# A Trainium2 layer kernel: its neighbourhood attention in units of one head and two query rows, on 64x64 and 64-column tiles of TensorE, with probabilities divided by GpSimd before they are transposed

## The reference

```python
def row_block(r):
    rs = r_start[r]          # clip(r - 4, 0, 32 - 8)
    ...
    s_loc = jnp.einsum('bjhd,bajchd->bhjac', q_r, k_r).astype(jnp.float32) * scale + bias.astype(jnp.float32)
    s_ctx = jnp.einsum('bjhd,blhd->bhjl', q_r, k_ctx).astype(jnp.float32) * scale
    s = jnp.concatenate([s_loc.reshape(b_, h_, GRID_W, n_loc), s_ctx], axis=-1)
    p = jax.nn.softmax(s, axis=-1).astype(v.dtype)
    p_loc = p[..., :n_loc].reshape(b_, h_, GRID_W, kr, WIN_C)
    return (jnp.einsum('bhjac,bajchd->bjhd', p_loc, v_r)
            + jnp.einsum('bhjl,blhd->bjhd', p[..., n_loc:], v_ctx))
```

## Time and profile before

| | before |
|---|---|
| median of 3 runs | 3817.42 us (3816.41 to 3820.98) |
| profiled execution, span from first to last instruction | 3823.5 us |
| profiled execution, own time beside the span | not given |
| TensorE busy in it | 3659.4 us, 96% |
| VectorE, ScalarE, GpSimd busy | 61%, 43%, 22% |

### The profile page before, as it was taken

How to read it: one execution, slowest core, us unless ns; L and a number is a source line. 1 busy time by engine, 2 the same in 40 slices (tenths; PEclk the granted TensorE clock), 3 DMA queues, 4 the chain that set the end, 5 groups by cost and what they waited for, 6 DMA issues and landing times. The chain is left out here.

```text
span 3823.5 us, 58042 instructions
## 1 busy us (share of the span) xinstructions
PE 3659.4 (96%) x19520; PEld 2936.9 (77%) x19520; DVE 2323.0 (61%) x3546; ACT 1645.7 (43%) x3006; POOL 856.0 (22%) x812
## 2 busy tenths in 40 slices
PE   8999999999997999989999999996799999999998
PEld 3444459986777999968888888785688888888887
DVE  4655632555656999953534353444767777677775
ACT  4333333334654666642424332322344445444452
POOL 3888500011106666610000000000000010000100
PEclk9999999999999999989999999997899999999999
DMA  7455455131115433344535352443477676766763
GB/s 283 155 144 142 119 182 130 57 86 45 26 46 183 125 118 122 96 160 125 177 105 170 99 172 73 152 154 130 145 214 226 214 220 206 214 224 215 219 209 92
DMA packets 258768, 570.97 MB, mean 149 GB/s; under 512 B 38971, under 2 KB 117339, under 8 KB 256347
## 3 DMA queue, kind: packets, MB, share of 16 engines
q1 hardware_dynamic: 225612, 451.18, 37.2%
q0 software_dynamic: 33040, 118.25, 10.4%
HBM read 458.27 MB, written 100.73 MB: 146 GB/s over the span
## 5 line engine op out<-in xcount | busy, mean ns | idle before, releaser
L3072 DVE TENSOR_TENSOR sb_we_low<-sb_we,sb_we_high 128x1024 fp32r<-128x1024 f32 x384 | 466.6, 1223 | 121.5 <-ACT sb_we_high L3023 121.5
L3023 ACT ACTIVATE sb_we_high<-sb_we 128x1024 fp32r<-128x1024 f32 x377 | 392.2, 1048 | 142.3 <-PE ey L2987 142.3
L2430 DVE TENSOR_TENSOR sb_wm_low<-sb_wm,sb_wm_high 128x1024 fp32r<-128x1024 f32 x127 | 155.4, 1224 | 393.6 <-ACT sb_wm_high L2340 393.6
L344 PE MATMUL p_ps<-sb_hT,sb_ring 128*128 128x512 f32 (+1 forms) x960 | 373.2, 549 | 0.0
L344 PEld LDWEIGHTS p_ps<-sb_hT,sb_ring 128*128 128x128 f32 x960 | 181.9, 190 | 186.2 <-issue 181.3
L2281 PE MATMUL pg<-sb_hb_high,sb_wm_high 128*128 128x512 f32 x768 | 303.3, 395 | 8.7 <-DVEq L2402 4.6
L2282 PE MATMUL pg<-sb_hb_low,sb_wm_high 128*128 128x512 f32 x768 | 300.4, 391 | 0.0
L2283 PE MATMUL pg<-sb_hb_high,sb_wm_low 128*128 128x512 f32 x768 | 300.1, 391 | 0.0
L2970 PE MATMUL eg<-sb_xe_parts,sb_we_high 128*128 128x512 f32 x1024 | 260.5, 396 | 1.6 <-DVE sb_xe_parts L3067 1.6
L2970 PE MATMUL eu<-sb_xe_parts,sb_we_high 128*128 128x512 f32 x1024 | 259.1, 395 | 0.0
L2932 POOL DMA_INDIRECT out<-sb_ybe,sb_ti x32 | 51.0, 1595 | 880.7 <-DVE sb_ybe L3107 822.7
(11 more groups left out here) (418 smaller groups left out, 8675.7 us busy)
## 6 DMA issues: line engine op xcount, KB each, us to landing
sb_we<-in_w_ex SPq DMA_DIRECT2D x384, 512.0 KB, 4.5
sb_wm<-in_w_gates SPq DMA_DIRECT2D x96, 512.0 KB, 3.6
sb_stage<-in_w_mod_row POOLq DMA_DIRECT2D x64, 256.0 KB, 3.6
sb_stage<-h_d SPq DMA_DIRECT2D x32, 512.0 KB, 4.3
sb_wm<-in_w_br SPq DMA_DIRECT2D x32, 512.0 KB
sb_ring<-in_w_ch POOLq DMA_DIRECT2D x19, 512.0 KB, 5.2
sb_gr<-gc_d SPq DMA_DIRECT2D x36, 256.0 KB, 3.8
sb_lk<-k_d SPq DMA_DIRECT2D x36, 256.0 KB, 4.0
```

Of the source, the lines that this page charges most:

```text
L344: last = nc.tensor.matmul(ps[:, b % BANKS, 0:wd], w[:, kind, k], hT[:, k, t0:t0 + wd], start=(k == 0), stop=(k == KD - 1))
L2430: v.tensor_tensor(wl[n], w[n], wh[n], ALU.subtract).then_inc(s.wl, 1)
L3023: nc.scalar.activation(wh[:, n % CUT], w[:, n % RAW], ACT.Copy).then_inc(s.wh, 1)
L3072: v.tensor_tensor(wl[:, n % CUT], w[:, n % RAW], wh[:, n % CUT], ALU.subtract).then_inc(s.wl, 1)
```

## The change

A unit becomes one head and two grid rows of queries (`j` = 0, 1); four units, the heads, make a pair of rows, and TensorE works on two of them, a pair `p` of heads, at a time. There are again 64 units, in 32 pairs, all unrolled. For each pair:

- `scores`: the queries go in as they are, as weights of 64 channels x 64 queries. A matmul for each head (`e`, partitions 64 e to 64 e + 63 of the input) and row (`j`, partitions 64 j to 64 j + 63 of the output), once for the local keys (512 columns, each row with its own window) and once for the context (256). GpSimd's doubled queries go.
- The scores are made negative (the query norm's factor and the bias table change sign), so that the maximum becomes a minimum. VectorE's `local` adds the bias and keeps the minimum in one instruction (in two halves where the two rows have different windows), `context` does the same for the context scores with a zero, straight from PSUM, and starts from the minimum of `local`. The exponential is taken in place with scale -1.
- GpSimd multiplies the 768 probabilities by the reciprocal of their sum (`sa.nm`), and TensorE's transposes wait for that.
- `turn`: four transposes for each unit into `turned`, then two each for the context of both units into `ctx_turned`. ScalarE copies the former (`copy_pt`), VectorE the latter for both units in one (`copy_ctx`).
- `values`: the values are the weights (128 keys x 64 channels) and the transposed probabilities of one row move (64 columns), so that the output comes out with its channels on partitions: 24 instructions a unit. The output's transposes, the scaling and the copies of quadrants go; ScalarE makes one copy a pair (`out`).
- There are four buffers for scores instead of two and two; the bias table holds each head for both rows (eight loads instead of four, four additions of the mask instead of two); a pair of grid rows is stored by two DMAs.
- `inner(0)` stands before the last pair's values.

The diff, cut to what is added; what it replaces stands in the functions above, and lines marked with a minus are kept where they are short:

```diff
@@ -671,11 +671,13 @@
...
+    UNITS = ROWS // 2 * H
+    PAIRS = UNITS // 2
...
+    BUF = 4
+    LK = KT - CT
@@ -685,53 +687,27 @@
...
+    def rows_of_unit(U):
+        i = U // 4
+        starts = [min(max(r - WR // 2, 0), ROWS - WR) for r in (2 * i, 2 * i + 1)]
+        return i, starts, [WR - 1 - (2 * i + j - starts[j]) for j in range(2)]
+    def edge(U):
+        _, _, shifts = rows_of_unit(U)
+        return shifts[0] != shifts[1]
+    def added(U):
+        return sum(2 if edge(x) else 1 for x in range(U))
...
+        area = sbuf(nc, c, "area", [P, 4976])
...
+        mx = sbuf(nc, c, "mx", [P, BUF, 4])
+        none = sbuf(nc, c, "none", [P, 1])
@@ -740,10 +716,11 @@
...
+        oc = sbuf(nc, c, "aoT", [P, 2, H, GRID])
...
+        sa = sems(nc, c, "at", "pad z zero rp sk bt0 sc lm cm ex rc nm tp tpc pt ptc o oe st0 st1")
@@ -772,10 +749,8 @@
...
+        sb = flat_ring[:, 0:BUF * KEYS].rearrange("p (u k) -> p u k", u=BUF)
+        bt = area[:, 1136:4976].rearrange("p (a r c) -> p a r c", a=H, c=GRID)
@@ -784,6 +759,7 @@
...
+        pt = FREE[:, 14336:14336 + 2 * KEYS].rearrange("p (u n c) -> p u n c", u=2, n=KT)
@@ -797,7 +773,8 @@
...
+        loc, cx, turned, po = bank[:, 0:2], bank[:, 2:4, 0:CTX], bank[:, 4:6], bank[:, 7, 0:2 * GRID].rearrange("p (u t) -> p u t", u=2)
+        ctx_turned = bank[:, 6].rearrange("p (u n c) -> p u n c", u=2, n=CT)
@@ -829,8 +806,8 @@
...
-                    half = h % 2
-                    sp.dma_start(bt[half * GRID:(half + 1) * GRID, h // 2], src).then_inc(sa.bt0, 16)
+                    for j in range(2):
+                        sp.dma_start(bt[j * GRID:(j + 1) * GRID, h], src).then_inc(sa.bt0, 16)
@@ -842,16 +819,16 @@
...
-                dst = g.oc_d.rearrange("(q p) (r t) -> p r q t", q=HP, t=GRID)
...
-                def store(i, odd):
-                    r = 2 * i + odd
-                    sp.wait_ge(sa.ote, 2 * (4 * i + 2 * odd + 2))
-                    sp.dma_start(dst[:, bass.ds(r, 1)].rearrange("p r q t -> p (r q) t"), oc[:, odd]).then_inc(s_st[odd], 16)
+                dst = g.oc_d.rearrange("(h c) (r t) -> c r h t", c=DH, t=GRID)
+                def store(i):
+                    sp.wait_ge(sa.oe, 2 * (i + 1))
+                    for j in range(2):
+                        sp.dma_start(dst[:, 2 * i + j], oc[j * DH:(j + 1) * DH, i % 2]).then_inc(s_st[i % 2], 16)
...
+                    store(n)
@@ -864,6 +841,7 @@
...
+                nc.gpsimd.memset(none[:], 0.0).then_inc(sa.zero, 1)
@@ -877,17 +855,10 @@
...
+                for U in range(UNITS):
+                    u = U % BUF
+                    pool.wait_ge(sa.rc, U + 1)
+                    nc.gpsimd.tensor_scalar(sb[:, u], sb[:, u], mx[:, u, 3:4], 1.0, ALU.mult, ALU.mult).then_inc(sa.nm, 1)
@@ -977,57 +948,59 @@
...
+                def scores(p):
+                    i, starts, _ = rows_of_unit(2 * p)
+                    hp = p % 2
+                    wait(pe, sa.lm, added(2 * p))
+                    for e in range(2):
+                        half = slice(e * DH, (e + 1) * DH)
+                        for j in range(2):
+                            at = CTX + starts[j] * GRID
+                            nc.tensor.matmul(loc[j * GRID:(j + 1) * GRID, e, 0:LOC], g.qn[half, hp, (2 * i + j) * GRID:(2 * i + j + 1) * GRID],
+                                             g.kn[half, hp, at:at + LOC], start=True, stop=True)
+                    if p == 0:
...
+                    wait(pe, sa.cm, 2 * p)
+                    for e in range(2):
+                        half = slice(e * DH, (e + 1) * DH)
+                        for j in range(2):
+                            nc.tensor.matmul(cx[j * GRID:(j + 1) * GRID, e], g.qn[half, hp, (2 * i + j) * GRID:(2 * i + j + 1) * GRID],
+                                             g.kn[half, hp, 0:CTX], start=True, stop=True).then_inc(sa.sc, 1)
+                def turn(p):
+                    for e in range(2):
+                        U = 2 * p + e
+                        pe.wait_ge(sa.nm, U + 1)
+                        for n in range(LK):
+                            last = nc.tensor.transpose(turned[:, e, n * P:(n + 1) * P], sb[:, U % BUF, n * P:(n + 1) * P], g.ident)
...
+                    for e in range(2):
+                        for n in range(CT):
+                            at = (LK + n) * P
+                            last = nc.tensor.transpose(ctx_turned[:, e, n], sb[:, (2 * p + e) % BUF, at:at + P], g.ident)
+                    last.then_inc(sa.tpc, 1)
+                def values(p):
+                    pe.wait_ge(sa.ptc, p + 1)
+                    wait(pe, sa.oe, p)
+                    for e in range(2):
+                        U = 2 * p + e
+                        _, starts, _ = rows_of_unit(U)
+                        cols = slice(U % 4 * DH, (U % 4 + 1) * DH)
+                        pe.wait_ge(sa.pt, U + 1)
+                        for n in range(KT):
+                            for j in range(2):
+                                rs = starts[j]
+                                if n >= LK:
+                                    v = vb[:, n - LK, cols]
+                                elif rs % 2:
+                                    v = v1[:, rs // 2 + n, cols]
+                                else:
+                                    v = vb[:, CT + rs // 2 + n, cols]
+                                last = nc.tensor.matmul(po[j * DH:(j + 1) * DH, e], v, pt[:, e, n, j * GRID:(j + 1) * GRID],
+                                                        start=(n == 0), stop=(n == KT - 1))
+                                if n == KT - 1 and e == 1:
+                                    last.then_inc(sa.o, 1)
@@ -1071,17 +1044,20 @@
...
+                scores(0)
+                scores(1)
...
+                for p in range(PAIRS):
+                    turn(p)
+                    if p + 2 < PAIRS:
+                        scores(p + 2)
+                    if p == PAIRS - 1:
+                        pe.wait_ge(sf.re, 16 * 2 * N2)
+                        pe.wait_ge(sa.cm, UNITS)
+                        inner(0)
+                    values(p)
@@ -1143,49 +1119,22 @@
...
+                def exps(U):
+                    act.wait_ge(sa.cm, U + 1)
+                    a(sb[:, U % BUF], sb[:, U % BUF], ACT.Exp, bias=mx[:, U % BUF, 1:2], scale=-1.0,
+                      accum_out=mx[:, U % BUF, 2:3]).then_inc(sa.ex, 1)
+                def copy_pt(U):
+                    act.wait_ge(sa.tp, U + 1)
+                    wait(act, sa.o, 2 * (U // 2))
+                    a(pt[:, U % 2, 0:LK], turned[:, U % 2].rearrange("p (n c) -> p n c", c=P), ACT.Copy).then_inc(sa.pt, 1)
+                def out(p):
+                    i, hp = p // 2, p % 2
+                    act.wait_ge(sa.o, 2 * (p + 1))
+                    if hp == 0:
+                        wait(act, s_st[i % 2], 32 * (i // 2))
+                    a(oc[:, i % 2, 2 * hp:2 * hp + 2], po, ACT.Copy).then_inc(sa.oe, 1)
@@ -1241,14 +1190,20 @@
...
+                for U in range(3):
+                    exps(U)
...
+                for p in range(PAIRS):
+                    copy_pt(2 * p)
+                    copy_pt(2 * p + 1)
+                    if p > 0:
+                        out(p - 1)
+                    for U in (2 * p + 3, 2 * p + 4):
+                        if U < UNITS:
+                            exps(U)
...
+                out(PAIRS - 1)
@@ -1323,7 +1278,7 @@
...
-                        v.tensor_scalar(nw[:, 0:1], nw[:, 0:1], DH ** -0.5, None, ALU.mult).then_inc(sm.rec, 1)
+                        v.tensor_scalar(nw[:, 0:1], nw[:, 0:1], -DH ** -0.5, None, ALU.mult).then_inc(sm.rec, 1)
@@ -1338,32 +1293,35 @@
...
+                def local(U):
+                    u = U % BUF
+                    _, _, shifts = rows_of_unit(U)
+                    dve.wait_ge(sa.sc, 4 * (U // 2 + 1))
+                    wait(dve, sa.tpc, (U - BUF) // 2 + 1)
+                    parts = [(0, P, shifts[0])] if not edge(U) else [(j * GRID, (j + 1) * GRID, shifts[j]) for j in range(2)]
+                    for lo, hi, dr in parts:
+                        v.tensor_tensor_reduce(sb[lo:hi, u, 0:LOC], loc[lo:hi, U % 2, 0:LOC], bt[lo:hi, U % 4, dr:dr + WR].rearrange("p r c -> p (r c)"),
+                                               1.0, 3e38, ALU.add, ALU.min, mx[lo:hi, u, 0:1]).then_inc(sa.lm, 1)
+                def context(U):
+                    u = U % BUF
+                    dve.wait_ge(sa.lm, added(U + 1))
+                    v.tensor_tensor_reduce(sb[:, u, LOC:KEYS], cx[:, U % 2], none[:].broadcast_to([P, CTX]),
+                                           1.0, mx[:, u, 0:1], ALU.add, ALU.min, mx[:, u, 1:2]).then_inc(sa.cm, 1)
+                def inverse_sum(U):
+                    u = U % BUF
...
                     v.reciprocal(mx[:, u, 3:4], mx[:, u, 2:3]).then_inc(sa.rc, 1)
...
+                def copy_ctx(p):
+                    dve.wait_ge(sa.tpc, p + 1)
```

(69 more changed lines are left out.)

146 lines of the change are left out of this document (1 added, 145 removed).

## The result

| | before | after |
|---|---|---|
| median, on the same chip, 4 runs each | 3818.62 us (3816.41 to 3820.98) | 3750.01 us (3745.48 to 3753.30) |
| profiled execution, own time | not given | 3748.97 us |
| its span | 3823.5 us | 3747.4 us |
| first matmul of the stage behind the attention | 1166.59 us | 1095.96 us |

The ratio is 0.9817, with a 95% interval of 0.9805 to 0.9829: 68.6 us, or 1.8%, **faster**. All of the gain is in the attention: the next stage's first matmul comes 70.6 us earlier. (The granted clock, averaged over the span, is 0.977 before and 0.976 after.)

The account below looks back on a forecast made before the run. It took TensorE to bound the kernel before and the ring to set the new pace: 32 x 8.26 = 264 against 243, 21 us more, plus 4 at the start, on 3817.4, gives 3842 us; range 3772 to 3885.

Parts of the forecast that it names:

- The ring: Waits through TensorE's transposes and scores, VectorE's logits and reciprocal, GpSimd's multiply: sets the pace, 2.90 + S + G = 8.26 us a pair.
- S: TensorE's score matmuls on 64x64 tiles: starting in program order, overlapping only between neighbouring tiles, 3.1 us a pair.
- rival C: TensorE's scores: all four 64x64 tiles run at once, 1.34 us a pair, total 3786 us; chance 0.30.
- G: GpSimd's multiply of 768 columns by the reciprocal, scaled from L294's 512 columns: 2.26 us a unit.
- rival B: GpSimd's normalisation is cheap, 0.82 us, so TensorE's 8.0 us a pair binds: 3832 us; chance 0.16.
- V: TensorE's 48 value instructions a pair at 0.062 us each: 3.0 us, hidden beside the ring.
- rival C with cheap normalisation: Scores on four tiles at once and GpSimd's multiply at 0.82: TensorE's 6.2 us a pair binds, 3776 us.
- 0.19 us for a change of shape: TensorE's cost of switching tile shape, three times a pair (transposes, scores, values): 0.57 us a pair.
- Edge units: hidden too: VectorE's split local add in the few edge units: hidden, no cost.
- Ends: Start of the attention: the first pair's transposes come some 4 us later than before, +4 us.
- The `zin` loads: Loads queued behind output stores, wanted some 8 us after issue: 0, or 1 to 2 us if late.
- The registers' 0.4 us a unit: Addresses worked out in registers on TensorE's queue slow 44 of the 64 units by 0.4 us each.

Follow-up runs that it names:

- e1: The changed kernel with GpSimd's multiplication given one operator instead of two: 3795.74 us, ratio 0.9928 to the kernel before.
- e4: The changed kernel with VectorE's reciprocal for unit 2p+3 moved ahead of the logits of units 2p+4 and 2p+5: 3731.34 us, ratio 0.9765 to the kernel before.
- e8: The changed kernel without GpSimd's multiplication, transposes waiting for the exponential alone, output not normalised: 3729.94 us, ratio 0.9765 to the kernel before.
- e9: The changed kernel with each pair's sixteen score instructions issued twice into the same places: 3795.54 us, ratio 0.9936 to the kernel before.
- e10: The changed kernel with scores issued twice and GpSimd's multiplication given one operator: 3838.89 us, ratio 1.0051 to the kernel before.
- e3: The changed kernel with each 64x64 tile's local and context scores next to each other, tile after tile: 3752.19 us, ratio 0.9816 to the kernel before.
- e7: The kernel before with its hardware loop over 44 units written out: 3802.2 us, ratio 0.9955 to the kernel before.
- e2: The changed kernel with the value matmuls' loops exchanged, all twelve of one row, then the other's: 3752.4 us, ratio 0.9819 to the kernel before.
- e6: e4 with all 32 zin loads issued ahead of all stores on SyncE's queue: 3767.16 us, ratio 0.9858 to the kernel before.
- e11: e4 with the zin loads issued two steps ahead of the stores: 3725.86 us, ratio 0.9750 to the kernel before.

## Why the prediction was wrong

- **The ring: right.** e1, e4, e8, e9 and e10 each move the pace as it says, and TensorE waits for GpSimd in 31 of 32 pairs. The fixed part came out at 5.05 - 1.45 - 0.91 = 2.69 instead of 2.90. The pair shown above places the difference: the transposes with what lies before the scores take 1.02 (983.93 to 984.95; predicted 1.05), the hand-over to VectorE 0.22 (0.16), and from L1303's start to GpSimd's it is 1.40 (981.57 to 982.97) where the prediction has 1.59. The reads of the accumulator, for which it added 0.08 each, hardly lengthen the chain.
- **"Only the second of one tile and the first of the next can overlap", S = 3.1: the step that failed.** It is 1.45, rival C's 1.34 plus 0.11. The assumption was that instructions start in program order; e3 shows that they don't. In program order stands the issue of instructions, not their start on separate tiles. The Trainium skill (TensorE: Matmul & The Clock Gate, Part 3) says that matmuls start and end strictly in order, which the prediction read as agreeing with it; e3's starts speak against it for separate tiles. The Trainium skill (TensorEngine Tiling (Array Packing), Key Properties) says that tiles work in parallel, and the four starts within 0.04 us bear it out. This was 1.65 us a pair, 53 us.
- **"The same operation over 512 columns", G = 2.26: failed too.** L294 has one operator; the change has two, and that is another price, 0.91 (e1). The prediction saw the second operator, in rival B, and set it aside for the row. The row was of another form. Another 1.35 us a pair, 43 us. The Trainium skill (GPSIMD Engine Reference, Engine selection) has an operation with one input at roughly line rate; that fits the 0.91, near the 0.82 of the copy's rate, and not the 2.20.
- **V = 3.0, beside the ring: hidden, as said, but mis-sized.** It is 1.55: the two column tiles run at once, 0.058 us for two instructions. Had it been 3.0, TensorE's sum would have been 0.93 + 0.53 + 1.45 + 3.0 = 5.9 and would have set the pace in place of the ring. That is why rival C with cheap normalisation, closest to what happened, still gave 3776 and not 3750.
- **"0.19 us for a change of shape", 0.57 a pair: somewhat too high.** In e4, where TensorE has no gap, twelve transposes with what lies before the scores take 1.46 us, 1.30 of it their own streams; S has 0.11 beyond 1.34, and V 0.16 beyond 24 steps of 0.058. All three changes together are thus 0.43 a pair at most, and no run separates them from the rest in it.
- **"Edge units: hidden too": wrong, a small term.** VectorE's split add is on the ring, and five steps take 5.77 us instead of 5.05: 3.6 us.
- **Ends: +4 at the start, measured +4.5: right by luck.** The prediction's sum, 885.6 + 3.1 + 3 x 1.27 + 2 x 0.16 + 2.26, comes to 895.1, 3.4 us behind 891.7; with the measured S and G it would be 892.1, 0.4 us. TensorE's timeline has other terms:

```profile
883.89 1.09 PE L959 MATMUL mix_ps<-sb_kn,sb_qn 64*64 64x512 f32 x8
889.05 1.98 PE L959 MATMUL mix_ps<-sb_kn,sb_qn 64*64 64x512 f32 x8 [3.64 <-DVE sb_mx L1303]
891.82 1.11 PE L975 MATMUL mix_ps<-sb_consts_sb,sb_ring 128*128 128x128 f32 x4
895.11 1.12 PE L975 MATMUL mix_ps<-sb_consts_sb,sb_ring 128*128 128x128 f32 x4 [2.18 <-POOL sb_ring L861]
```

The scores start 1.8 us earlier than before, since nothing waits for doubled queries. But PSUM holds the scores of one pair, so those of the second wait 3.64 us for VectorE's adds, which are split in two for these first pairs; then the clock is at its lower level (0.50 from 889 to 895 us), and GpSimd is waited for again. The prediction had none of these three.
- **The `zin` loads: wrong.** They were put at "0, or 1 to 2 us if late" and cost 4.80 us of idle time and 1.8 us of lower clock behind it. The 8 us that the last loads have before they are wanted were taken from a pace of 8 us a pair; at 5.05 they were no longer there.
- **The registers' 0.4 us a unit: right** (e7, 0.41).
- **The chances.** C had 0.30 and B 0.16, as if they excluded each other; both were true at once, and the range's foot (3772) took C and B together but with the price of V that neither questioned. Two of its sums leave out the 4 us of the start: B with free changes of shape is 3815 and not 3811, and the foot should be its own 3776.

Putting the two measured prices into the prediction's own ring gives 32 x 5.26 = 168 against 243, and with +4 for the start 3746 us; with the wait at the tail, 3753. The kernel took 3750. Some of that closeness is balance: the ring is 0.21 us a pair too long (7 us), and the pairs with two windows (3.6) and the inner transform that moved (2.2 less) are not in it.

## What to carry to other kernels

Before an instruction's price is scaled from another row, compare its form: the number of operators, where its scalar comes from, its tile; e1 shows a factor of 2.4 between a multiply alone and one with an operator more that multiplies by 1. A kernel that works in small tiles should give consecutive instructions to different tiles, and not more than a few in a row to one (four cost nothing in e3, twelve cost 0.85 us a pair in e2). When the pace is set by a loop of waits through several engines, look for the cheapest instruction that stands in it only by program order: here a 0.16 us reciprocal, moved ahead of the logits, was worth 19 us. Loads queued behind stores need a lead that is checked anew when the pace changes.

## What the runs showed of the hardware that was not expected

- Sixteen fp32 score instructions on four 64x64 tiles take 1.45 us, against 5.36 one after another (worked out from the prices of the full-array instructions); order by tile (e3) doesn't matter for four in a row, but costs 0.85 us for twelve (e2).
- GpSimd's multiply of 128x768 by a number per partition: 0.91 us with two operators, 2.20 with one (e1), with no spread.
- 32 loads issued back to back on one queue took 1.8 us each to issue instead of 0.44, and held the stores behind them for 58 us (e6).
- The clock fell to its lower level after 4.8 us of idle time at the tail, and the first four 512-column instructions behind it took 3.68 us instead of 1.98 (after, e4); with the wait gone it did not fall there (e11).
